# Running sums of squares of the norms: added by GpSimd instead of the vector engine, in a hybrid decoder layer on one core

## The chip, the core and the metric

The kernel runs on one core of a Trainium2 chip. The core has a matrix engine (TensorE, in the profile PE, its weight loads PEld), a vector engine (VectorE, DVE), an activation engine (ScalarE, ACT), a general engine (GpSimd, POOL) and a queue for transfers (SyncE, SP). Each engine works through its own list of instructions in order and waits only at semaphores. Operands lie in SBUF (128 partitions), products of TensorE in PSUM. The metric is the time of one execution on the device in microseconds; less is better.

## What is computed

One layer on 1056 tokens (1024 of a prompt, 8 x 4 new ones) with 1024 features: a feed-forward block, a mixer of two head groups (convolution and linear recurrence), a second feed-forward block, and a gated input embedding. Each block has an RMS norm before and after it.

```python
def rmsnorm(x, g):
    y = xf * lax.rsqrt(jnp.mean(xf * xf, axis=-1, keepdims=True) + EPS)
    return (y * g.astype(jnp.float32)).astype(x.dtype)

def decoder_layer(...):
    x = x + 0.5 * rmsnorm(swiglu_ffn(rmsnorm(x, ffn1_pre_g), ...), ffn1_post_g)
    x, ... = mixer_block(x, ...)      # pre2, conv norm, post2 inside: x + rmsnorm(out, post_g)
    x = x + 0.5 * rmsnorm(swiglu_ffn(rmsnorm(x, ffn2_pre_g), ...), ffn2_post_g)
    gate = jax.nn.sigmoid(rmsnorm(x, ple_norm_g) @ ple_w_gate)
    e = p @ ple_w_proj
    return x + rmsnorm(gate * e, ple_post_g)
```

## The kernel before

**Tiling.** Features lie on the partitions (8 tiles of 128), tokens along the free dimension in three chunks c = 0, 1, 2 of C = 352. Every tensor of x is 128 x 8 x 1056. All products are made in three passes (`passes`, L589 to L591) of a high and a low part, so each activation exists as `x_hi` (a rounded copy, ScalarE) and `x_lo` (the rest, VectorE), and each weight block as `w_hi` (ScalarE, L1022 or L1018) and `w_lo` (VectorE, L1503 or L1498).

**A norm.** A norm of one chunk needs the mean of squares over all features. ScalarE squares tile after tile (`square`, L1048): the first tile goes straight into the running sum `ssum[:, i % 2]`, the others into a ring `sq` of SQ = 3 buffers, so that square m waits for add m-3. `add_square` (L1526) adds each of them to the sum. TensorE adds over the partitions (`norm_sum`, L628), ScalarE takes the root (L1057), VectorE the reciprocal (`invert`, L1541), TensorE spreads it to all partitions (`norm_spread`, L640), and ScalarE copies it to `rstd_pre` or `rstd_post` (L1065). TensorE makes products between these steps. There are 27 norms, in the order of the table `NORMS`: pre1, then post1 and pre2, conv, post2 and pre3, post3 and pre4, post4, each for three chunks. They have 8 tiles (conv: 4), so 177 adds. Each add waits for its square and for the add before it; the counters `sq_done` and `add_done` run through all norms.

**Where VectorE makes the adds.** For pre1 it alternates `x_lo` (L1757) and an add. For a post-norm it makes the 7 adds in one row (`add_squares`), in the FFN's last step after the 8 sums of the chunk (`down`, L1650, acc = ps + acc). The pre-norm behind a post-norm is computed in `apply_pair`, four times per chunk, two tiles each: acc times rstd (L1554), times gain plus x_hi (L1559, twice), plus x_lo (L1563); then ScalarE makes the new x_hi (L1077) and squares the two tiles, and VectorE makes x_lo of the pair before (L1568) and the adds of that pair; in the last call it also serves its own pair. Where the next step of the program is a unit of the mixer, of w_out or of the gate, the calls stand between the units' instructions (gelu_in L2035, oc, L2154 and L2163). All these orders are written out by hand.

**GpSimd** makes three constants and the identity at the start (L565 to L569), then nothing.

**Waits on TensorE's side.** `norm_sum` waits for `add_done` to reach the last add of its norm, `norm_spread` for the reciprocal. Both stand in TensorE's list among the products, so a late add holds up all products behind it. `start_products` of chunk c waits tile by tile for x_lo.

Of the kernel before, what the change touches and what calls it, by code (L numbers as in the profile page):

```python
# [23 lines left out]
ALU = mybir.AluOpType  # L24
# [6 lines left out]
NJ = 4  # L31
# [16 lines left out]
SQ = 3  # L48
# [83 lines left out]
NORM = {(n, c): i for i, (n, c, _) in enumerate(NORMS)}  # L132
TILES = [t for _, _, t in NORMS]
BEHIND = [i for i, (n, _, _) in enumerate(NORMS) if not n.startswith("pre")]
SQ0 = [sum(TILES[:i]) for i in range(len(TILES) + 1)]
ADD0 = [sum(t - 1 for t in TILES[:i]) for i in range(len(TILES) + 1)]
# [55 lines left out]
def build(nc, a, out):  # L192
    ctx = ExitStack()
    with ctx:
# [24 lines left out]
        ssum = tile("ssum", [P, 2, C])  # L219
        std = tile("std", [P, 8])  # L220
        sq, sq_at, _ = place("sq", [P, SQ, C])
# [341 lines left out]
        @block.gpsimd  # L563
        def _(eng):
            eng.memset(ident[:, :], 0.0).then_inc(const_ready, 1)  # L565
            eng.memset(ones[:, :], 1.0).then_inc(const_ready, 1)
            eng.memset(eps_t[:, :], EPS).then_inc(const_ready, 1)
            eng.wait_ge(const_ready, 3)
            eng.affine_select(out=ident[:, :], in_=ident[:, :], compare_op=ALU.not_equal, fill=1.0,  # L569
                              base=0, pattern=[[-1, P]], channel_multiplier=1  # L570
                              ).then_inc(const_ready, 1)

# [891 lines left out]
        def _(eng):  # L1466
# [51 lines left out]
                eng.tensor_tensor(wd_lo[:, :], rawd[:, :], f32(wd_hi[:, :]), ALU.subtract  # L1518
                                  ).then_inc(down_lo, 1)

            def add_square(i, m):

                eng.wait_ge(sq_done, SQ0[i] + m + 1)
                if ADD0[i] + m - 1 > 0:
                    eng.wait_ge(add_done, ADD0[i] + m - 1)
                eng.tensor_tensor(ssum[:, i % 2, :], ssum[:, i % 2, :], sq[:, (ADD0[i] + m - 1) % SQ, :],  # L1526
                                  ALU.add
                                  ).then_inc(add_done, 1)

            def add_squares(name, c):  # L1530
                i = NORM[name, c]
                for m in range(1, TILES[i]):
                    add_square(i, m)

            def invert(name, c):

                i = NORM[name, c]
# [11 lines left out]
            def apply_pair(post, c, x0, src, gain, pre, q):  # L1549

                r, m, two = rstd(post, c), 2 * q, src(c, 2 * q, 2)
                n = mark(eng.tensor_tensor(two, two, r.unsqueeze(1).broadcast_to([P, 2, C]),  # L1554
                                           ALU.mult))
                eng.wait_ge(dve_own, n)
                for h in range(2):
                    t = src(c, m + h)[:, 0, :]
                    n = mark(eng.scalar_tensor_tensor(t, t, gain(m + h),  # L1559
                                                      f32(x_hi[:, m + h, cols(c)]),  # L1560
                                                      ALU.mult, ALU.add))
                eng.wait_ge(dve_own, n)
                eng.tensor_tensor(two, two, f32(x_lo[:, m:m + 2, cols(c)]), ALU.add  # L1563
                                  ).then_inc(x_new if pre else y_fin, 1)
                for p in ((q - 1, q) if q == 3 else (q - 1,)):
                    if pre and p >= 0:
                        eng.wait_ge(x_hi_done, x0 + PAIRS * c + p + 1)
                        eng.tensor_tensor(x_lo[:, 2 * p:2 * p + 2, cols(c)], src(c, 2 * p, 2),  # L1568
                                          f32(x_hi[:, 2 * p:2 * p + 2, cols(c)]), ALU.subtract
                                          ).then_inc(x_lo_done, 1)  # L1570
                        for k in (2 * p, 2 * p + 1):
                            if k:
                                add_square(NORM[pre, c], k)

            def scaled(f, i, c, h, up):

# [98 lines left out]
            def ffn_last(f, post, pre, x0):  # L1675


                i = NI - 1
                for c in range(NC):
                    def pair(q):  # L1680
                        if c:
                            apply_pair(post, c - 1, x0, acc_tile, half_gain(f), pre, q)

                    def hook(at):
                        if c == 0 and at == "g0":
                            split_down(i + NI * f)
                        if c and at == "g1":
                            invert(*((post, 0) if c == 1 else (pre, 0)))
                        if c == 2 and at == "u0":
                            invert(post, 1)  # L1690
                    hidden_chunk(f, i, c, tiles(f, i), hook)
                    pair(0)
                    for m in range(KT):
                        down(f, i, c, m)
                        if m in (2, 5, 7):
                            q = 1 + (2, 5, 7).index(m)
                            pair(q)
                            if c == 2 and q > 1:
                                for k in range(4):
                                    tiles(f, i)(1, 4 * (q - 2) + k)  # L1700
                    if (f, c) != (1, 2):
                        add_squares(post, c)

            def p_to_features():
                for c in range(NC):
# [46 lines left out]
            for c in range(NC):  # L1752
                i = NORM["pre1", c]
                for k in range(KT):
                    n = RING["xT", c, k]
                    eng.wait_ge(sq_done, SQ0[i] + k + 1)
                    eng.tensor_tensor(x_lo[:, k, cols(c)], ps[:, n % BANKS, 0:C],  # L1757
                                      f32(x_hi[:, k, cols(c)]), ALU.subtract
                                      ).then_inc(psum_free, 1)
                    eng.wait_ge(psum_free, n + 1)  # L1760
                    if k:
                        add_square(i, k)
                if c == 0:
                    vectors()
                    split_wide(0)
                    split_wide(1)
                invert("pre1", c)
                hidden_chunk(0, 0, c, tiles(0, 0),
                             lambda at: (c, at) == (2, "g0") and split_down(0))
# [300 lines left out]
            for n in range(12):  # L2070
# [10 lines left out]
                gelu_in(n)  # L2081
                if n:
                    yb(n - 1)
                if part == 1:
                    for j in range(1, NJ):
                        add_square(NORM["conv", c], j)
                if part == 3:
                    invert("conv", c)
                if part == 0 and c:
# [16 lines left out]
            for c in range(NC):  # L2106
                for q in range(4):
# [6 lines left out]
                        out_pair(c - 1, q - 1)  # L2114
                    if c and q == 3:
                        out_pair(c - 1, 3)
                add_squares("post2", c)


            def hook(c, at):  # L2120
# [49 lines left out]

            ple_unit(0, 0)
            invert("pre4", 1)
            add_squares("post3", 2)
            ple_unit(0, 1)
            invert("post3", 2)
            for q in range(4):
                apply_pair("post3", 2, 6 * PAIRS, acc_tile, half_gain(1), "pre4", q)
                ple_unit(*divmod(q + 2, 4))
            add_squares("post4", 0)
            ple_unit(1, 2)  # L2180
            invert("pre4", 2)
            ple_unit(1, 3)
# [1 line left out]
            ple_unit(2, 0)  # L2184
            finish(0, 0)
            finish(0, 1)
            add_squares("post4", 1)
            ple_unit(2, 1)
            invert("post4", 1)
            finish(0, 2)  # L2190
# [3 lines left out]
            finish(1, 0)  # L2194
            finish(1, 1)
            ple_unit(2, 3)
            add_squares("post4", 2)
            invert("post4", 2)
            finish(1, 2)
            finish(1, 3)  # L2200
# [41 lines left out]
```

## Time and profile before

| | |
|---|---|
| Time, median of 3 runs | 2345.52 us (2345.4 to 2349.55) |
| Profiled execution, span from the first to the last instruction | 2337.7 us |
| TensorE busy | 2158.0 us (92%), 13020 matmuls |
| VectorE busy | 1317.6 us (56%), 2620 instructions |
| ScalarE busy | 769.8 us (33%), 1500 instructions |
| GpSimd busy | 0.9 us, 8 instructions |
| Adds of the sums (L1526) | 92.6 us, 177 instructions |

The span is that of one profiled execution; the runs measure the whole execution on the device, so their median is 7.8 us above it. In the profile a row of instructions gives the start in us from the span's start, the time they took, engine, line, operation, output and inputs, shape and count; in brackets stands how long the engine had been idle before and what ended that. Equal instructions that follow each other are drawn together (x7), also where short gaps lie between them. "L1526" is a line of the kernel before; in the changed kernel the lines are other ones.

### The profile page before, as it was taken

The page shows a single profiled execution, that of the slowest core. Times are in us where ns is not written, and L with a number is a line of the kernel's source. Part 1 is how long each engine was busy: PE and PEld are TensorE (multiplying, and loading weights), DVE is VectorE, ACT ScalarE, POOL GpSimd, SP SyncE. Part 2 cuts the span into 40 slices and gives each one's busy share as a digit, 9 for nine tenths or more (in the row PEclk, how much of TensorE's full clock was granted, in tenths as well). Part 3 has the DMA queues.
Part 4 walks back from the last instruction along what each step waited for, and adds up shares of the span by engine and source line. Part 5 has one row for each costly group of instructions (what it writes and reads, how often), then busy time and mean ns, then how long its engine had stood idle before and what let it go on. Part 6 is the DMA issues. An engine that isn't in the chain of part 4 may idle for free. (4 is left out here: it accounts for less than half of the span.)

```text
span 2337.7 us, 34611 instructions
## 1 busy us (share of the span) xinstructions
PE 2158.0 (92%) x13020; PEld 2106.1 (90%) x13020; DVE 1317.6 (56%) x2620; ACT 769.8 (33%) x1500; POOL 0.9 (0%) x8
## 2 busy tenths in 40 slices
PE   5899999999999878999989689999999999995886
PEld 5899999999999878887789689999999999995886
DVE  4544444543445666988555764545434554557686
ACT  4311121221122333365575532212221121225563
POOL 0000000000000000000000000000000000000000
PEclk8999999999999889999999889999999999998897
DMA  4101111101111011100014201111101111102222
GB/s 149 37 28 45 54 54 54 54 27 35 45 54 54 1 45 41 46 1 19 19 38 144 91 1 55 55 54 54 45 18 45 54 54 54 54 1 73 72 91 75
DMA packets 92360, 116.15 MB, mean 50 GB/s; under 512 B 4596, under 2 KB 83704, under 8 KB 92282
## 3 DMA queue, kind: packets, MB, share of 16 engines
q1 hardware_dynamic: 91065, 110.79, 14.4%
q10 hardware_dynamic: 1216, 4.33, 0.6%
q8 instruction: 48, 0.79, 0.1%
q14 instruction: 31, 0.25, 0.0%
HBM read 110.15 MB, written 4.95 MB: 49 GB/s over the span
## 5 line engine op out<-in xcount | busy, mean ns | idle before, releaser
L589 PE MATMUL ps<-x_hi,w_lo 128*128 128x352 f32 x2688 | 883.2, 329 | 17.8 <-DVE w_lo L1503 8.8
L590 PE MATMUL ps<-x_lo,w_hi 128*128 128x352 f32 x2688 | 872.9, 325 | 0.0
L591 PE MATMUL ps<-x_hi,w_hi 128*128 128x352 f32 x2688 | 871.9, 324 | 0.0
L589 PEld LDWEIGHTS ps<-x_hi,w_lo 128*128 128x128 f32 x2688 | 514.6, 191 | 19.1 <-DVE w_lo L1503 9.5
L590 PEld LDWEIGHTS ps<-x_lo,w_hi 128*128 128x128 f32 x2688 | 515.3, 192 | 0.0
L591 PEld LDWEIGHTS ps<-x_hi,w_hi 128*128 128x128 f32 x2688 | 513.5, 191 | 0.0
L589 PE MATMUL ps<-a_hi,wd_lo 128*128 128x352 f32 x1104 | 361.6, 328 | 24.6 <-DVE a_lo L1600 11.6
L590 PE MATMUL ps<-a_lo,wd_hi 128*128 128x352 f32 x1104 | 357.7, 324 | 0.0
L591 PE MATMUL ps<-a_hi,wd_hi 128*128 128x352 f32 x1104 | 357.3, 324 | 0.0
L1650 DVE TENSOR_TENSOR acc<-ps,acc 128x352 f32<-128x352 f32 x480 | 249.3, 523 | 88.7 <-PE ps L591 82.8
L1583 DVE TENSOR_TENSOR tmp_u<-ps,rstd_pre 128x352 f32<-128x352 f32 x132 | 69.1, 524 | 370.7 <-PE ps L591 370.7
L1022 ACT ACTIVATE w_hi<-raw,params 128x256 fp32r<-128x256 f32 x512 | 213.6, 496 | 132.0 <-DMA raw<-in_ffn_w_gu_dram 109.1
L1503 DVE SCALAR_TENSOR_TENSOR w_lo<-raw,params,w_hi 128x256 fp32r<-128x256 f32 x512 | 225.8, 477 | 46.7 <-ACT w_hi L1022 46.7
L1089 ACT ACTIVATE tmp_s<-tmp_g 128x352 f32<-128x352 f32 x132 | 65.3, 498 | 552.1 <-DVE tmp_g L1583 552.1
L589 PEld LDWEIGHTS ps<-a_hi,wd_lo 128*128 128x128 f32 x1104 | 210.4, 191 | 27.6 <-DVE a_lo L1600 12.8
L590 PEld LDWEIGHTS ps<-a_lo,wd_hi 128*128 128x128 f32 x1104 | 210.9, 191 | 0.0
L591 PEld LDWEIGHTS ps<-a_hi,wd_hi 128*128 128x128 f32 x1104 | 210.1, 190 | 0.0
L1583 DVE TENSOR_TENSOR tmp_g<-ps,rstd_pre 128x352 f32<-128x352 f32 x132 | 68.5, 522 | 244.1 <-PE ps L591 230.0
L1098 ACT ACTIVATE a_hi<-tmp_a 128x352 fp32r<-128x352 f32 x132 | 59.9, 494 | 418.4 <-DVE tmp_a L1594 418.4
L829 PE MATMUL ps<-gp,diag 128*128 128x352 f32 (+1 forms) x360 | 108.8, 460 | 3.5 <-ACT diag L1284 3.5
L1526 DVE TENSOR_TENSOR ssum<-ssum,sq 128x352 f32<-128x352 f32 x177 | 92.6, 523 | 22.3 <-ACT sq L1048 9.5
L829 PEld LDWEIGHTS ps<-gp,diag 128*128 128x128 f32 x360 | 69.2, 194 | 38.1 <-issue 5.5
(172 smaller groups left out, 1678.2 us busy)
## 6 DMA issues: line engine op xcount, KB each, us to landing
raw<-in_ffn_w_gu_dram SPq DMA_DIRECT2D x88, 512.0 KB, 3.5
rawd<-in_ffn_w_down_dram SPq DMA_DIRECT2D x22, 1024.0 KB, 7.6
raw<-in_w_out_dram SPq DMA_DIRECT2D x24, 512.0 KB, 3.5
raw<-in_ple_w_gate_dram SPq DMA_DIRECT2D x24, 512.0 KB, 3.4
raw<-in_w_in_dram SPq DMA_DIRECT2D x16, 512.0 KB, 4.0
x_in<-in_x_prompt_dram ACTq DMA_DIRECT2D x6, 512.0 KB, 7.8
out_dram<-y_stage SPq DMA_DIRECT2D x6, 512.0 KB, 2.8
rawd<-in_ple_w_proj_dram SPq DMA_DIRECT2D x1, 1024.0 KB, 7.2
```

Source lines behind the costliest of these rows:

```text
L589: eng.matmul(dst, wl, xh, start=first, stop=False)
L590: eng.matmul(dst, wh, xl, start=False, stop=False)
L591: return eng.matmul(dst, wh, xh, start=False, stop=last)
L829: mm = eng.matmul(dst[:, 0:w], diag[:, tap, :], gp[:, j, at0:at0 + w], start=tap == 0, stop=tap == TP - 1)
L1022: ins = eng.activation(w_hi[s][:, sl], raw[:, sl], ACT.Copy, scale=vec(gain, k))
L1089: eng.activation(tmp_s[:, h, :], tmp_g[:, h, :], ACT.Silu).then_inc(silu_done, 1)
L1098: eng.activation(a_hi[:, h, cols(c)], tmp_a[:, h, :], ACT.Copy).then_inc(a_hi_done, 1)
L1503: ins = eng.scalar_tensor_tensor(w_lo[s][:, sl], raw[:, sl], vec(gain, k), f32(w_hi[s][:, sl]), ALU.mult, ALU.subtract)
L1526: eng.tensor_tensor(ssum[:, i % 2, :], ssum[:, i % 2, :], sq[:, (ADD0[i] + m - 1) % SQ, :], ALU.add).then_inc(add_done, 1)
L1583: eng.tensor_tensor((tmp_u if up else tmp_g)[:, h, :], src, rstd_pre[:, cols(c)], ALU.mult).then_inc(psum_free, 1)
L1650: eng.tensor_tensor(acc[:, m, cols(c)], src, acc[:, m, cols(c)], ALU.add).then_inc(psum_free, 1)
```

## The change

`add_square` moves to the GpSimd program, which gets one loop over all norms and tiles behind its constants. All calls of it on VectorE go, the function `add_squares` too, and with the calls in pre1 the wait of VectorE for its own x_lo. The semaphores and their counts are the same, so squares, sums and products wait for the same events.

```diff
 @block.gpsimd
+            def add_square(i, m):
+
+                eng.wait_ge(sq_done, SQ0[i] + m + 1)
+                if ADD0[i] + m - 1 > 0:
+                    eng.wait_ge(add_done, ADD0[i] + m - 1)
+                eng.tensor_tensor(ssum[:, i % 2, :], ssum[:, i % 2, :], sq[:, (ADD0[i] + m - 1) % SQ, :],
+                                  ALU.add
+                                  ).then_inc(add_done, 1)
+
+            for i in range(len(NORMS)):
+                for m in range(1, TILES[i]):
+                    add_square(i, m)
 @block.vector
-            def add_square(i, m):
-            def add_squares(name, c):
...
 def apply_pair
-                        for k in (2 * p, 2 * p + 1):
-                            if k:
-                                add_square(NORM[pre, c], k)
 def ffn_last
-                    if (f, c) != (1, 2):
-                        add_squares(post, c)
 pre1
-                    eng.wait_ge(psum_free, n + 1)
-                    if k:
-                        add_square(i, k)
 conv norm
-                if part == 1:
-                    for j in range(1, NJ):
-                        add_square(NORM["conv", c], j)
 mixer, gated embedding
-                add_squares("post2", c)
-            add_squares("post3", 2)
-            add_squares("post4", 0)
-            add_squares("post4", 1)
-            add_squares("post4", 2)
```

VectorE's list at the end of the first FFN, chunk 1, from the second `apply_pair` to the next products of the hidden layer, before:

```order
L1568 TENSOR_TENSOR x_lo<-acc,x_hi 128x2x352
L1526 TENSOR_TENSOR ssum<-ssum,sq 128x352 x2
L1650 TENSOR_TENSOR acc<-ps,acc 128x352 x2
L1554 TENSOR_TENSOR acc<-acc,rstd_post 128x2x352
L1559 SCALAR_TENSOR_TENSOR acc<-acc,half_g,x_hi 128x352 x2
L1563 TENSOR_TENSOR acc<-acc,x_lo 128x2x352
L1568 TENSOR_TENSOR x_lo<-acc,x_hi 128x2x352
L1526 TENSOR_TENSOR ssum<-ssum,sq 128x352 x2
L1568 TENSOR_TENSOR x_lo<-acc,x_hi 128x2x352
L1526 TENSOR_TENSOR ssum<-ssum,sq 128x352 x9
L1583 TENSOR_TENSOR tmp_g<-ps,rstd_pre 128x352 x2
```

and now:

```order
L1567 TENSOR_TENSOR x_lo<-acc,x_hi 128x2x352
L1646 TENSOR_TENSOR acc<-ps,acc 128x352 x2
L1553 TENSOR_TENSOR acc<-acc,rstd_post 128x2x352
L1558 SCALAR_TENSOR_TENSOR acc<-acc,half_g,x_hi 128x352 x2
L1562 TENSOR_TENSOR acc<-acc,x_lo 128x2x352
L1567 TENSOR_TENSOR x_lo<-acc,x_hi 128x2x352 x2
L1579 TENSOR_TENSOR tmp_g<-ps,rstd_pre 128x352 x2
```

The adds are gone from between the x_lo, and the nine at the end (two of pre2, seven of post1) no longer stand ahead of tmp_g. Near the end of the program, from the last unit of the gated embedding to the first pair behind the last norm, VectorE's list before:

```order
L2154 TENSOR_TENSOR acc<-ps,rstd_pre 128x352 x2
L2163 TENSOR_TENSOR acc<-ps,acc 128x352 x2
L1526 TENSOR_TENSOR ssum<-ssum,sq 128x352 x7
L1541 RECIPROCAL std<-std 128x3
L1554 TENSOR_TENSOR acc<-acc,rstd_post 128x2x352
```

and GpSimd's list now, from its last constant to its end:

```order
L567 MEMSET eps_t 128x1
L569 ISA
L569 AFFINE_SELECT ident<-ident 128x128
L578 TENSOR_TENSOR ssum<-ssum,sq 128x352 x177
L194 UNCONDITIONAL_BRANCH
```

VectorE's reciprocal now follows the unit directly and waits there for the sum, with the applies queued behind it as before; the adds stand in a list that holds nothing else.

## Rows read from the trace of the kernel before

**Rows 1.** The page: busy time of TensorE; its busy tenths and granted clock in 40 slices.
```profile
PE 2158.0 (92%) x13020; PEld 2106.1 (90%) x13020; DVE 1317.6 (56%) x2620; ACT 769.8 (33%) x1500; POOL 0.9 (0%) x8
...
PE   5899999999999878999989689999999999995886
...
PEclk8999999999999889999999889999999999998897
```

**Rows 2.** Adds (L1526) in five stretches: sum of the stretches, sum of busy time.
```profile
sum 785.00, DVE 92.62; mean DVE 18.52
```

**Rows 3.** Who waits for whom, TensorE: us in total, times, longest.
```profile
PE ps_aux L628 <- DVE ssum L1526: 71.9, 10, 11.8
```

**Rows 4.** Instructions of VectorE by form: busy us, mean ns, idle before.
```profile
L1650 DVE TENSOR_TENSOR acc<-ps,acc 128x352 f32<-128x352 f32 x480 | 249.3, 523 | 88.7 <-PE ps L591 82.8
...
L1526 DVE TENSOR_TENSOR ssum<-ssum,sq 128x352 f32<-128x352 f32 x177 | 92.6, 523 | 22.3 <-ACT sq L1048 9.5 <-DVE ssum L1526 0.9
...
L1554 DVE TENSOR_TENSOR acc<-acc,rstd_post 128x704 f32<-128x704 f32 x44 | 38.8, 882 | 7.9 <-ACT rstd_post L1065 7.9
```

**Rows 5.** GpSimd in order of time, two of its eight instructions.
```profile
0.74 0.20 POOL L565 MEMSET ident<- 128x128 f32 x1 [0.29 <-POOLq L2230]
...
1.35 0.29 POOL L569 TENSOR_SCALAR_AFFINE_SELECT ident<-ident 128x128 f32<-128x128 f32 x1 [0.23 <-POOL eps_t L567]
```

**Rows 6.** In order of time, pre1 chunk 1: ScalarE, VectorE, TensorE.
```profile
49.84 0.49 ACT L1190 ACTIVATE x_hi<-ps 128x352 fp32r<-128x352 f32 x1
50.52 0.51 ACT L1190 ACTIVATE x_hi<-ps 128x352 fp32r<-128x352 f32 x1
...
51.03 0.52 DVE L1526 TENSOR_TENSOR ssum<-ssum,sq 128x352 f32<-128x352 f32 x1
...
52.03 0.52 DVE L1526 TENSOR_TENSOR ssum<-ssum,sq 128x352 f32<-128x352 f32 x1
...
53.09 0.63 PE L589 MATMUL ps<-x_hi,w_lo 128*128 128x352 f32 x1 [1.18 <-DVE x_lo L1757]
```

**Rows 7.** In order of time, pre2 chunk 0: VectorE, ScalarE, TensorE.
```profile
797.33 0.52 DVE L1526 TENSOR_TENSOR ssum<-ssum,sq 128x352 f32<-128x352 f32 x1
797.76 1.38 DVE L1650 TENSOR_TENSOR acc<-ps,acc 128x352 f32<-128x352 f32 x3
...
802.70 1.15 DVE L1526 TENSOR_TENSOR ssum<-ssum,sq 128x352 f32<-128x352 f32 x2
803.76 0.95 DVE L1650 TENSOR_TENSOR acc<-ps,acc 128x352 f32<-128x352 f32 x2
...
810.14 5.55 DVE L1526 TENSOR_TENSOR ssum<-ssum,sq 128x352 f32<-128x352 f32 x9
...
808.28 1.04 ACT L1048 ACTIVATE sq<-acc 128x352 f32<-128x352 f32 x2
...
810.75 3.64 ACT L1048 ACTIVATE sq<-acc 128x352 f32<-128x352 f32 x6 [0.66 <-DVE ssum L1526]
...
818.40 0.26 ACT L1057 ACTIVATE std<-ps_aux,eps_t 128x3 f32<-128x3 f32 x1
...
811.34 1.44 PE L628 MATMUL ps_aux<-ones,ssum 128*128 128x1 f32 x6 [6.12 <-DVE ssum L1526]
...
819.37 0.81 PE L640 MATMUL ps_aux<-ident,std 128*128 128x128 f32 x6
```

**Rows 8.** In order of time, TensorE: behind pre2 chunk 2, behind conv chunk 1.
```profile
891.72 0.66 PE L589 MATMUL ps<-x_hi,w_lo 128*128 128x352 f32 x1 [6.16 <-DVE x_lo L1568]
...
1195.69 1.60 PE L640 MATMUL ps_aux<-ident,std 128*128 128x128 f32 x6 [5.77 <-DVE std L1541]
```

**Rows 9.** In order of time, TensorE: the sum of post3 chunk 2.
```profile
2178.25 1.44 PE L628 MATMUL ps_aux<-ones,ssum 128*128 128x1 f32 x6 [3.98 <-DVE ssum L1526]
```

**Rows 10.** In order of time, VectorE: the adds of post4 chunk 1.
```profile
2272.76 4.29 DVE L1526 TENSOR_TENSOR ssum<-ssum,sq 128x352 f32<-128x352 f32 x7
```

**Rows 11.** In order of time, VectorE: the adds of the last norm.
```profile
2305.49 4.30 DVE L1526 TENSOR_TENSOR ssum<-ssum,sq 128x352 f32<-128x352 f32 x7 [0.18 <-ACT sq L1048]
```

More of the change, by code:

```diff
@@ L1519, in split_down @@
                                   ).then_inc(down_lo, 1)
-            def add_square(i, m):
[L1523 to L1528, printed above, removed]
-            def add_squares(name, c):
-                i = NORM[name, c]
-                for m in range(1, TILES[i]):
-                    add_square(i, m)
             def invert(name, c):
```

## Prediction

> **What bounds the kernel now.** I read the page first, then who waits for whom on TensorE, then the instructions in order of time around those waits. TensorE is busy for 2158 of 2337.7 us, and its slices are at 9 or more except at the start, in slices 14 to 16, 21 to 24 and 37 to 40; the granted clock (PEclk) falls in most of the same slices [rows 1]. All adds lie in five stretches around these, together 785 us [rows 2]; the long loops of the two FFNs hold none. So the loops can't move, and the change is decided in the five stretches. There the largest single wait of TensorE is for the last add of a sum: 71.9 us in 10 waits [rows 3]. An add costs the vector engine 523 ns, 92.6 us for 177 of them [rows 4]. What matters is how much of these lies on a chain that TensorE waits for. All times below are walked from the trace of this one execution.
>
> **The price of an add on GpSimd.** No row shows it. GpSimd runs 8 instructions before, all at the start; the nearest are a memset of 128x128 in 0.20 us and a select over 128x128, which reads one operand, in 0.29 us [rows 5]. By length (352/128) they give 0.55 and 0.80 us. An add reads two operands; at worst the reads follow each other, 1.6 us. I take 0.9, nearest to the select, and a hand-off to the next add (each waits for the one before) of 0.1 as on the vector engine, where nine adds take 5.55 us, a pitch of 0.63 against 0.525 busy [rows 4, 7]. Pitch 1.0 us, ends 0.65 and 1.7.
>
> **Do the two engines hinder each other?** No row shows GpSimd beside the vector engine. The price is bounded below by nothing and above by one whole add for each add that meets a vector instruction with two SBUF operands. The vector engine takes 523 ns for an add of two SBUF tiles and 523 ns for one with a PSUM operand [rows 4], so it draws two SBUF streams at full rate; the question is whether GpSimd's two streams fit beside them. I take it that they don't and that the engines take turns, instruction by instruction: a third reader that needs two streams of its own is more likely to cost something than nothing, and the applies are made of just such instructions. Instructions with a PSUM operand run freely beside an add. The Trainium skill, "SBUF — State Buffer", section "Who interferes with whom", says the same in stronger words: a vector instruction with two SBUF inputs and a GpSimd instruction that reads SBUF exclude each other for the whole instruction. No run here shows it yet; if it is wrong, rival 1 is the sum.
>
> **Start: -1.7.** In chunks 1 and 2 of the first norm the vector engine alternates x_lo and add, 0.99 us per tile, while ScalarE makes a copy and a square in 0.69, and TensorE waits for x_lo before its products [rows 6]. These x_lo read PSUM and one SBUF tile, so there are no turns. Without the adds x_lo follows ScalarE. TensorE needs the first four x_lo; they come 1.0 us earlier in chunk 1 and 0.7 in chunk 2. The squares now wait for GpSimd (three buffers: square m waits for add m-3), at 1.0 per tile, no slower than 0.99 before. In chunk 0 the wait for parameters hides everything.
>
> **The nine pre-norm sums.** One walked, chunk 0 of pre2 [rows 7]. Removed from the vector engine ahead of the last pair's squares: one add and a pair, 0.43 and 1.06 of pitch = 1.49. Put in: adds 1 to 5 run on GpSimd as soon as their squares are there. Add 1 meets an apply, 0.9; of the pair 2, 3 and the pair 4, 5 one each hides under the L1650 instructions that read PSUM, and the others cost 0.75 and 0.6. Together 2.25 - 1.49 = +0.8. At the end: the two last squares finish at 809.3 + 0.8 = 810.1; GpSimd waits for the x_lo instruction that holds SBUF until 810.05 and adds twice, 812.1, against 811.3 before. TensorE's wait so ends 0.8 later. Then comes the post-norm behind it: its last square waits for its add 4, at 812.1 + 4.0, ends at 816.6 against 814.4, and ScalarE's silu and root stand behind it on its queue (a table load, silu and a second load; some 0.5 us of the delay is absorbed where silu waited for its input). The root comes at 820.1 instead of 818.4, the reciprocal at 820.6, and TensorE's spread at 820.8 instead of 819.4: **+1.4**. The same walk for the others with TensorE or its inputs waiting gives +1.5 and +1.2 in chunks 1 and 2 of pre2, +2.0, +2.1 and +0.9 for pre3, +2.0 and +1.7 for pre4 chunks 0 and 1; eight in all, +12.8. They differ by what covers the adds: a wait for w_hi covers some in chunk 1, nothing covers those of chunk 2, where TensorE waits for x_lo itself [rows 8]. The ninth, pre4 chunk 2, is made while the gate units run: its adds fall under sigmoids and PSUM readers, and the freed vector engine releases the next unit earlier, -2.6.
>
> **The conv norms: -1.3.** Three adds of 1.0 end 1.2 us later than three of 0.6, once on TensorE's path; but the y_lo and w_lo behind them on the vector engine start up to 1.7 us earlier, and TensorE waits for that chain 5.77 us before the next spread [rows 8]. In all -2.6 without turns; w_lo reads two SBUF tiles, which takes half of it back.
>
> **Post-norm sums of the last stage.** Where all squares are ready and nothing hides the adds, seven cost 7.0 instead of 4.3 us, +2.7. That is so for post3 chunk 2, where TensorE waits 3.98 us [rows 9], and for post4 chunk 2, the last norm of the kernel: add, sum, root, reciprocal, spread, applies and stores all stand in one chain behind it [rows 11]. In post4 chunk 0 the next unit is released 0.3 earlier. In post4 chunk 1 the seven adds stood behind two pairs of applies [rows 10]. They now start at 2266.6 instead of 2272.8, but run in turns with the applies, 5.7 us of two-operand instructions; six turns of 0.9 push the applies to 2278.2, and the unit behind them starts 1.2 later. Sum: 2.7 + 2.7 - 0.3 + 1.2 = +6.3. Queues: only GpSimd's gets work, nothing but adds, and in the order in which they ran before, so no norm is held up by a foreign one. The DMA queues of SP and ScalarE are not touched; ScalarE's squares wait for other times, which is counted above. Further shares of the 92.6 us lie in waits of the vector engine and bring nothing.
>
> **Sum:** -1.7 + 12.8 - 2.6 - 1.3 + 6.3 = +13.5 us. Span 2337.7 + 13.5 = 2351.2; the median of the runs is 7.8 above this span, so 2359. Per 0.1 us of pitch the sum moves by about 5 us (four post adds or two last adds in each of eight walks, and 2 x 7 at the end), since the last add is on the chain.
>
> **Rivals.** 1: *No hindrance.* The same walks with free adds: eight pre-norm sums -8.5, the ninth -2.8, conv -2.6, post3 +2.7, post4 -0.8, -4.0 and +2.7, start -1.7: -15, time 2330.5. Here the result is faster; it turns at a pitch of about 1.35 us. For it speaks that vector instructions keep 514 to 528 ns here while TensorE and ScalarE read SBUF beside them; against it, that neither of these reads as the vector engine does. 2: *Long adds.* A pitch of 1.6 or more (two reads one after the other, or a slow start of each instruction): the sum of the forecast + 6 x 5 = +43, time 2389. Against it speaks the select's 0.29. 3: *Nothing to measure.* Turns, but with a pitch near 0.8, or half as many collisions: the sum is 0 to +4, about 2347. The gains in the chunks where TensorE waits 6 to 12 us and the longer sums cancel. 4: *GpSimd starves.* If the vector engine's next instruction always goes first, the applies run as in rival 1, and the adds follow in one row at their end: three to four late adds in each of the eight walks, about +2.2 each, +18 in all with the end, 2364. It lies inside the forecast's band.
>
> **How the numbers follow.** Forecast with its neighbour 4: 0.58 (2352 to 2375). No hindrance: 0.22 (2324 to 2338). Nothing to measure: 0.13. Long adds: 0.07. About 0.2%, 4.7 us, is what a measurement of this kernel can tell from no change. Slower holds 0.56 of the first case, 0.07 of the long adds and 0.01 of the third; faster holds 0.21 of the second and 0.02 of the third; the rest is same. The whole range is 2327 to 2380: it reaches into both neighbours and leaves out the lower end of rival 1 and the long adds. The forecast's own range is 2350 to 2378.
>
> **What would show it.** Adds on GpSimd with a start-to-start spacing of 1.0 us, TensorE's waits for ssum near 85 us instead of 71.9. If the turns are real, the mean of L1554, L1563 and L1568 grows or gaps of up to 0.9 us open ahead of them, and L1650 keeps its 523 ns; if not, they stay at 0.88 us and the applies end 1.5 us earlier in each chunk. The last sum of the kernel must be 2.7 us longer in any case, and TensorE's products of chunks 1 and 2 must start about 1 us earlier. The forecast is wrong if the engines don't meet, or if the pitch is far from 1.0.

## The result, and the profile after

| | before | after |
|---|---|---|
| Time, median of 9 runs each | 2344.41 us (2335.91 to 2349.55) | 2355.28 us (2352.43 to 2363.84) |
| Span of the profiled execution | 2337.7 us | 2352.4 us |
| TensorE busy | 2158.0 us | 2162.9 us |
| VectorE busy | 1317.6 us | 1256.6 us |
| GpSimd busy | 0.9 us | 181.8 us |

The ratio of the times is 1.0054, 95% interval [1.0039, 1.0069]: about 12.7 us slower, between 9 and 16. Here and below, microseconds beside a ratio are the ratio times the median of the runs of before that it was measured against; the two medians of the table are 10.9 us apart. The two profiled executions are 14.7 us apart. The page of the changed kernel, busy time, then GpSimd's slices and the clock granted to TensorE:

```profile
PE 2162.9 (92%) x13020; PEld 2109.1 (90%) x13020; DVE 1256.6 (53%) x2443; ACT 766.8 (33%) x1500; POOL 181.8 (8%) x185
...
POOL 2100000000000230000012310000000000022131
PEclk8999999999999989999999799999999999997897
```

GpSimd works where the five stretches of [rows 2] lie, and nowhere else. VectorE lost 61 us of busy time, not the 92.6 us of its adds: 31.6 us are missing. Added up one by one, its 2443 other instructions take 26.6 us longer than before; the other 5 us are overlaps of neighbouring rows, which busy time counts once. 16.5 of the 26.6 us are to be seen in the instructions on `acc` (line, engine, form, count: min/median/max in ns, first and last start), which answer to [rows 4], with GpSimd's adds above them:

```profile
L578 POOL TENSOR_TENSOR ssum<-ssum,sq x177: 923/943/1987, 11.6 to 2323.5; 128x352 f32<-128x352 f32 x177
```
```profile
L1646 DVE TENSOR_TENSOR acc<-ps,acc x480: 510/524/526, 167.6 to 2159.3; 128x352 f32<-128x352 f32 x160
...
L1558 DVE SCALAR_TENSOR_TENSOR acc<-acc,half_g,x_hi x48: 571/584/1257, 784.2 to 2241.5; 128x352 f32<-128x352 f32 x48
L1553 DVE TENSOR_TENSOR acc<-acc,rstd_post x44: 858/884/1633, 783.3 to 2340.5; 128x704 f32<-128x704 f32 x44
L1562 DVE TENSOR_TENSOR acc<-acc,x_lo x44: 891/892/1524, 785.3 to 2342.6; 128x704 f32<-128x704 f32 x44
```

An add on GpSimd takes 0.93 us where it is alone. VectorE's instructions with two SBUF operands keep their medians, but their longest are 0.63 to 0.75 us above them (the longest L1554 before was 893 ns). The w_lo made of two SBUF tiles do the same (L1516: median 476 ns, longest 1199). L1646, which reads PSUM, has no long one among 480. So some instructions wait, each by up to most of one add.

TensorE's waits, the answer to [rows 3] (us in total, times, longest):

```profile
PE ps_aux L641 <- POOL ssum L578: 85.2, 13, 12.2
```

Chunk 0 of pre2, the answer to [rows 7], GpSimd first, then VectorE, ScalarE and TensorE:

```profile
797.80 2.48 POOL L578 TENSOR_TENSOR ssum<-ssum,sq 128x352 f32<-128x352 f32 x2 [3.09 <-ACT sq L1061]
803.38 6.63 POOL L578 TENSOR_TENSOR ssum<-ssum,sq 128x352 f32<-128x352 f32 x6 [3.09 <-ACT sq L1061]
```
```profile
798.10 1.40 DVE L1553 TENSOR_TENSOR acc<-acc,rstd_post 128x704 f32<-128x704 f32 x1
799.54 1.63 DVE L1558 SCALAR_TENSOR_TENSOR acc<-acc,half_g,x_hi 128x352 f32<-128x352 f32 x2
```
```profile
805.79 0.50 ACT L1061 ACTIVATE sq<-acc 128x352 f32<-128x352 f32 x1 [0.57 <-POOL ssum L578]
...
810.62 1.28 ACT L1102 ACT_TABLE_LOAD   x1
...
814.11 0.26 ACT L1070 ACTIVATE std<-ps_aux,eps_t 128x3 f32<-128x3 f32 x1
```
```profile
805.75 1.44 PE L641 MATMUL ps_aux<-ones,ssum 128*128 128x1 f32 x6 [6.70 <-POOL ssum L578]
814.63 0.91 PE L653 MATMUL ps_aux<-ident,std 128*128 128x128 f32 x6 [0.76 <-DVE std L1540]
```

Two adds that met applies took 2.48 us, the first six of a row of nine (two of pre2, seven of post1) 6.63. L1553 took 1.40 instead of 0.88. The sum waited 6.70 us instead of 6.12. Then ScalarE's squares of the post-norm behind (five of them alike) each wait 0.57 to 0.59 us for an add, since a square may only be written when the add three before it is done. Silu and root stand behind them on the same queue, and the spread comes when the root does.

The two ends that nothing covers, TensorE at post3 chunk 2 [rows 9] and GpSimd's adds of the last norm [rows 11]:

```profile
2191.56 1.44 PE L641 MATMUL ps_aux<-ones,ssum 128*128 128x1 f32 x6 [7.06 <-POOL ssum L578]
```
```profile
2317.09 7.34 POOL L578 TENSOR_TENSOR ssum<-ssum,sq 128x352 f32<-128x352 f32 x7 [30.53 <-ACT sq L1061]
```

7.06 us of waiting instead of 3.98, and seven adds in 7.34 us instead of 4.30.

**How the traces are compared below.** Each norm has a sum and a spread on TensorE (L628 and L640 before). The start of each, minus its start in the trace of before, is a shift; where the shift grows, time is lost between this step and the one before it. A shift belongs to two executions.

### The profile page after: what moved, and what is told of

The parts are those of the page before. It is cut to its first block and busy times, and to the rows that moved or that the text cites. A ratio compares the mean times of both kernels' runs of the same rounds, so it can differ in the third digit from the quotient of the medians.

```text
span 2352.4 us, 34607 instructions
## 1 busy us (share of the span) xinstructions
PE 2162.9 (92%) x13020; PEld 2109.1 (90%) x13020; DVE 1256.6 (53%) x2443; ACT 766.8 (33%) x1500; POOL 181.8 (8%) x185
## 5 line engine op out<-in xcount | busy, mean ns | idle before, releaser
L578 POOL TENSOR_TENSOR ssum<-ssum,sq 128x352 f32<-128x352 f32 x177 | 180.9, 1022 | 2141.9 <-ACT sq L1061 2123.7
L1646 DVE TENSOR_TENSOR acc<-ps,acc 128x352 f32<-128x352 f32 x480 | 249.3, 523 | 87.1 <-PE ps L604 81.2
L1516 DVE SCALAR_TENSOR_TENSOR w_lo<-raw,params,w_hi 128x256 fp32r<-128x256 f32 x512 | 229.1, 484 | 53.5 <-ACT w_hi L1035 53.5
L602 PEld LDWEIGHTS ps<-a_hi,wd_lo 128*128 128x128 f32 x1104 | 210.4, 191 | 24.8 <-DVE a_lo L1596 12.8
L641 PEld LDWEIGHTS ps_aux<-ones,ssum 128*128 128x128 f32 x162 | 27.3, 247 | 88.8 <-POOL ssum L578 88.8
```

Source lines behind the costliest of these rows:

```text
L602: eng.matmul(dst, wl, xh, start=first, stop=False)
L641: mm = eng.matmul(ps_aux[:, n % 2, q:q + 1], ssum[:, i % 2, t0:t0 + P], ones[:, 0:1], start=True, stop=True)
L1516: ins = eng.scalar_tensor_tensor(w_lo[s][:, sl], raw[:, sl], vec(gain, k), f32(w_hi[s][:, sl]), ALU.mult, ALU.subtract)
L1646: eng.tensor_tensor(acc[:, m, cols(c)], src, acc[:, m, cols(c)], ALU.add).then_inc(psum_free, 1)
```

## Experiments

The theory going in: what is lost is lost because each GpSimd add is longer, where it stands at the end of a chain, and because the two engines take turns when both read SBUF. Rivals: only the length matters; only the clock differs; nothing adds up because what one step gives another takes.

All mixes but the three with extra work use one rule, with VectorE's calls in their places as before and the same semaphore counts (where pre1 is on GpSimd, VectorE's wait for its own x_lo goes with its adds). Squares, sums and products are the same whoever adds:

```diff
+def on_gpsimd(i, m):
+    name, c, _ = NORMS[i]
+    return <the rule of the experiment>
 @block.gpsimd
+            for i in range(len(NORMS)):
+                for m in range(1, TILES[i]):
+                    if on_gpsimd(i, m):
+                        add_square(i, m)
 @block.vector
             def add_square(i, m):
+                if on_gpsimd(i, m):
+                    return
```

### One part at a time

**The sums of pre2, pre3 and pre4 alone.** Rule: `name in ("pre2", "pre3", "pre4")`.

> Only the sums of pre2, pre3 and pre4 (nine norms, 63 of the 177 adds) are added by GpSimd, all others by the vector engine as before. Theory (turns): the two last adds of eight of these sums end 0.8 us later as in the walk of pre2 chunk 0, but the post-norm sum behind each keeps its pitch of 0.63 us, so less than the +1.4 to +2.1 per norm is left: 8 x 0.6 - 2.6 for the ninth = about +2 us, and the vector engine's two-operand instructions show maxima of 1.3 us and more. Rival (no hindrance, length of the adds alone): 8 x -1.1 - 2.8 = about -11 us. Rival (collisions are the whole loss): as much slower as the changed kernel, +11 us.

Measured: ratio 0.9997 [0.9985, 1.0009], -0.7 us. Neither -11 nor +11: near the theory, at its favourable side. VectorE's other instructions together take 15.5 us longer than before, so the collisions are there, and still nearly nothing is lost. In this -0.7 us the ninth sum, pre4 chunk 2, is included, at which the shift falls by 3.0 us (below). So the other eight cost about 2 us, give or take as much, where the theory had 8 x 0.6 = 4.8.

**All post-norms and conv norms.** Rule: `name in ("post1", "post2", "post3", "post4", "conv")`.

> The complement of e1 and e4: GpSimd adds the sums of all post-norms and conv norms (93 adds), the vector engine those of pre1 to pre4. If the parts add up, it costs what is left of the changed kernel's 12.7 us: 12.7 + 5.2 + 0.7 = +18.6 us. Theory (the post-norm's root is late where its adds stand behind the pre-norm's on GpSimd, and the last sums are longer; with the pre-norm's adds back on the vector engine the post-norm's start no later than before): post3 chunk 2 +3.1, the last norm +3.0 to 4.5, eight post-norms behind a pre-norm up to 1.5 each, conv -0.6: +8 to +18, below the sum of the parts. Rival (post-norm sums are hidden but for the two at the end): +6.

Measured: 1.0067 [1.0050, 1.0085], +15.7 us, about 12 to 20. That excludes the rival of +6. With pre1 alone (-5.2, below) and the pre-norms alone (-0.7) the three parts add up to 9.8 us, the whole change to 12.7 with an interval of 9 to 16, so they add up within the noise. The two traces show how the loss divides. Chunk 0 of pre2, sum and spread on TensorE, first with the pre-norm's adds on GpSimd alone, then with the post-norms' alone:

```profile
811.09 1.44 PE L647 MATMUL ps_aux<-ones,ssum 128*128 128x1 f32 x6 [5.99 <-POOL ssum L583]
819.08 0.80 PE L659 MATMUL ps_aux<-ident,std 128*128 128x128 f32 x6
```
```profile
807.60 1.44 PE L647 MATMUL ps_aux<-ones,ssum 128*128 128x1 f32 x6 [6.12 <-DVE ssum L1547]
816.49 0.91 PE L659 MATMUL ps_aux<-ident,std 128*128 128x128 f32 x6 [0.72 <-DVE std L1562]
```

From sum to spread it is 8.03 us before [rows 7], 7.99 with the pre-norms on GpSimd, 8.89 with the post-norms, 8.88 in the changed kernel. The same subtraction at the five places where a post-norm's squares lie between the two steps, in us against before:

| sum to spread | changed kernel | pre-norms alone | post-norms, conv alone |
|---|---|---|---|
| pre2 chunk 0 | +0.85 | -0.04 | +0.86 |
| pre2 chunk 1 | +1.49 | -0.30 | +1.81 |
| pre3 chunk 0 | +1.93 | -0.61 | +1.90 |
| pre3 chunk 1 | +1.27 | -0.02 | +1.26 |
| pre4 chunk 0 | +1.28 | +0.17 | +1.29 |
| sum | +6.8 | -0.8 | +7.1 |

The growth of the shift up to the six sums of pre2 and pre3 is +1.3 us in the changed kernel, +1.6 with the pre-norms alone and +0.3 with the post-norms alone. So the longer pre-norm sums cost some 1.5 us in all six, and almost five times as much is lost behind them, where the post-norm's adds lie. The way there is ScalarE: its rows of waits name the squares (us in total, times, longest), pre-norms alone, then post-norms and conv alone:

```profile
ACT sq L1067 <- POOL ssum L583: 3.3, 8, 0.6
```
```profile
ACT sq L1067 <- POOL ssum L583: 22.1, 38, 1.1
```

In the changed kernel it is 25.4 us in 46 waits. The total alone says little, for the squares waited before too, for VectorE's adds:

```profile
ACT sq L1048 <- DVE ssum L1526: 19.6, 15, 6.0
```

Of these 19.6 us, 13.7 lie in three long waits (near 771, 2071 and 2273 us), where VectorE made its adds only after other work; the changed kernel has no such wait longer than 1.1 us, but 24 of its 46, 13.4 us, lie at the five places of the table. There the squares of a post-norm that follow each other are paced by the adds, 1.07 us instead of 0.6, and the root of the pre-norm's sum stands behind them. The direct test, a ring of six square buffers under the changed kernel, wasn't made: it needs three more buffers of 1408 bytes per partition each. So ScalarE's part rests on these rows and on the mixes.

**The first norm alone.** Rule: `name == "pre1"`.

> Only the sums of pre1, the first norm (three chunks, 21 adds), are added by GpSimd. By the walk TensorE's products of chunks 1 and 2 start about 2 us earlier and nothing else changes: -2 us. If the fall of the granted clock behind the wait for wd_lo near 100 us is missing here too, as in the trace of the changed kernel, -6 us. Rival (what comes earlier is waited for elsewhere): 0.

Measured: 0.9978 [0.9966, 0.9991], -5.2 us. In the trace chunk 2's sum comes 2.3 us earlier (about 2 were expected), and at the first post-norm the shift is -6.3. The other 4.1 us arise where the clock differs. TensorE's work from 90 to 110 us by stretches (start:end, length, busy us of PE, PEld, DVE, ACT, POOL, granted clock, DMA share, GB/s), before and then in the changed kernel, where the shift falls by the same 4.1 us:

```profile
90.00:100.00 10.00, 7.36 (x47) 7.07 (x46) 3.64 (x4) 4.40 (x5) 0.00 (x0) 0.93 0.00 0
100.00:110.00 10.00, 10.00 (x49) 10.00 (x49) 8.27 (x21) 5.99 (x15) 0.00 (x0) 0.73 0.17 52
```
```profile
90.00:100.00 10.00, 7.36 (x48) 7.07 (x47) 4.08 (x5) 6.15 (x9) 0.00 (x0) 1.00 0.00 0
100.00:110.00 10.00, 10.00 (x63) 9.73 (x62) 10.00 (x25) 4.24 (x10) 0.00 (x0) 1.00 0.28 80
```

In both, TensorE waits 2.6 us once for wd_lo in the first stretch. Behind it the clock granted is 0.73 before (part of the stretch at 1.2 instead of 2.4 GHz, 49 matmuls in 10 us) and 1.00 in the changed kernel (63 matmuls). How much of the 4.1 us the change gives is open: with the pre-norms alone on GpSimd, where all work up to 778 us is that of before, the clock is 0.92 in the second stretch and the shift falls by 1.2 us too, and in the last mix below, which has pre1 on GpSimd, it falls by 2.8. The two traces of before are the slowest of all in this piece.

**The first norm and the ninth pre-norm.** Rule: `name == "pre1" or (name, c) == ("pre4", 2)`, 28 adds.

> Only the sums of pre1 and of pre4 chunk 2 (28 adds) are on GpSimd. Theory (steps add up, each where its own vector instructions are freed): the 5.2 us that pre1 alone gave, and 2.6 to 3.0 for the ninth pre-norm, whose step was -2.9 in the changed kernel and -3.0 with the pre-norm sums alone: about -8 us against the kernel before. Rival (what one gives is taken back by a lower clock or a later wait): -5 us or less.

Measured: 0.9959 [0.9944, 0.9975], -9.6 us. The shift falls by 3.0 us at the spread of pre4 chunk 2 (-2.3 to -5.3), as it does in the changed kernel (14.1 to 11.1) and with the pre-norms alone (7.5 to 4.5). The steps add up.

### The ends

**The last norm back on VectorE.** Rule: `(name, c) != ("post4", 2)`.

> As the changed kernel, but the seven adds of the very last norm (post4 chunk 2) are back on the vector engine. Theory: nothing covers this sum, 7 x (1.05 - 0.615) = 3.0 us come back, so 0.13% less than the changed kernel, +8 us against the kernel before. Rival (something else in the tail grew, 4.5 us between the last units of the two traces): all of 4.5 us comes back. Rival (the loss is only the clock's): nothing comes back.

Measured: 1.0036 [1.0022, 1.0049] against 1.0054: 4.2 us come back by the two ratios, though their intervals overlap. The adds are again a row of VectorE's, of the old length:

```profile
2315.77 4.30 DVE L1547 TENSOR_TENSOR ssum<-ssum,sq 128x352 f32<-128x352 f32 x7 [0.18 <-ACT sq L1067]
```

From the spread of post4 chunk 1 to the last sum the shift grows by 1.2 us here and by 4.6 in the changed kernel: 3.4 us are this norm's. The other 1.0 to 1.2 appears in the kernels with pre1 alone and with pre1 and the ninth too, which change nothing there. It belongs to the trace of before, not to the change.

**The last two adds of every sum on VectorE.** Rule: `m < TILES[i] - 2`.

> In every sum the last two adds are made by the vector engine, all before them by GpSimd. Theory (the last adds of a sum stand on the chain and cost 1.05 instead of 0.6 us each): 0.9 us for the pre-norm sum in each of nine places, and as much for post3 chunk 2 and the last norm, come back: about 10 us less than the changed kernel, about 0 against the kernel before. Rival (collisions with the applies are the loss): they remain, at most 3 us come back, +8 us against the kernel before.

Measured: 1.0068 [1.0049, 1.0087]: no less than the changed kernel. My expectation fell, though the part it was about came true. The sum of pre2 chunk 0 waits 5.99 us instead of 6.70. What I hadn't walked is the queue behind the waiting add. GpSimd, VectorE, TensorE:

```profile
805.18 5.24 POOL L583 TENSOR_TENSOR ssum<-ssum,sq 128x352 f32<-128x352 f32 x5 [4.76 <-DVE ssum L1547]
```
```profile
810.53 1.16 DVE L1547 TENSOR_TENSOR ssum<-ssum,sq 128x352 f32<-128x352 f32 x2 [5.49 <-POOL ssum L583]
```
```profile
805.09 1.44 PE L647 MATMUL ps_aux<-ones,ssum 128*128 128x1 f32 x6 [5.99 <-DVE ssum L1547]
...
814.92 0.91 PE L659 MATMUL ps_aux<-ident,std 128*128 128x128 f32 x6 [2.89 <-DVE std L1562]
```

VectorE stands still for 5.49 us for the post-norm's fifth add, with tmp_g behind it in its queue. So silu and the root come late, and the spread waits 2.89 us instead of 0.76. A chain split between two engines makes the one that comes second wait with all that it has queued.

### Do the engines hinder each other?

Three kernels keep all adds on VectorE and give GpSimd extra work that no one waits for, released by the same squares. `op` is an add, a copy (each writes bf16, since no space for 352 fp32 elements is free), or four memsets:

```diff
+            idle = 0
+            for i in range(len(NORMS)):
+                for m in range(1, TILES[i]):
+                    eng.wait_ge(sq_done, SQ0[i] + m + 1)
+                    if idle:
+                        eng.wait_ge(idle_done, idle)
+                    op(...).then_inc(idle_done, 1)
+                    idle += 1
```

> The kernel before, with all 177 adds on the vector engine, and GpSimd beside them makes one add more for each, of 352 elements that belong to nobody (two reads of the constants ident, a write to a spare tile), released by the same squares. No work waits for them. Theory (turns between instructions that read two SBUF operands): the vector engine's adds and applies show maxima of 0.5 to 0.75 us above their medians, and since the adds themselves collide now too, the time rises by about 15 us (5 to 30). Rival (only the length of GpSimd's adds on the chain matters): 0, within 2 us.

> As with the extra adds, but each extra instruction is a copy of 352 elements: one SBUF read instead of two. Theory in its narrow form (only an instruction with two reads hinders): 0, within 2 us. In its wide form (any read of GpSimd hinders): in proportion to its busy time, half of the extra adds or more, +5 us and above, and maxima in the same rows.

> As with the extra adds, but four memsets of 176 elements in place of each add: GpSimd is busy for about as long and reads no SBUF. Theory: 0, within 2 us, and the vector engine's maxima stay within 20 ns of their medians. Rival (GpSimd's writes, or its semaphore traffic, are what hinders): as much as the extra adds.

| extra work on GpSimd | GpSimd busy | VectorE busy, against before | ratio | us |
|---|---|---|---|---|
| 177 adds (two SBUF reads) | 182.9 us | +82.9 us | 1.0348 [1.0326, 1.0370] | +81.6 |
| 177 copies (one SBUF read) | 103.1 us | +20.9 us | 1.0070 [1.0053, 1.0088] | +16.4 |
| 708 memsets (no read) | 174.8 us | -0.3 us | 1.0003 [0.9989, 1.0018] | +0.7 |

VectorE's own adds (min/median/max in ns) beside the extra adds, the copies and the memsets:

```profile
L1546 DVE TENSOR_TENSOR ssum<-ssum,sq x177: 509/1061/1291, 12.3 to 2394.5; 128x352 f32<-128x352 f32 x177
```
```profile
L1544 DVE TENSOR_TENSOR ssum<-ssum,sq x177: 511/609/798, 12.3 to 2326.8; 128x352 f32<-128x352 f32 x177
```
```profile
L1552 DVE TENSOR_TENSOR ssum<-ssum,sq x177: 515/525/528, 12.4 to 2316.1; 128x352 f32<-128x352 f32 x177
```

The work of all other engines is the same in all three, and so are its waits and counts. GpSimd busy without reads costs nothing that can be measured; a single read stream costs; two cost most. A copy is also shorter than an add (GpSimd is busy for 103.1 instead of 182.9 us), so the second read and the length aren't separated. The rows of the applies beside the extra adds:

```profile
L1574 DVE TENSOR_TENSOR acc<-acc,rstd_post x44: 859/884/1646, 789.8 to 2411.7; 128x704 f32<-128x704 f32 x44
```

So the hindrance is real, and it hangs on GpSimd reading SBUF. That it goes by whole instructions in turn fits these maxima (an add of 0.93 us lengthens no apply by more than 0.76) but isn't separated from a slowing of both. The narrow form of my theory (only two reads hinder) fell. The wide one holds in kind, but not in size: the copies cost a fifth of what the adds cost, not half, at 0.56 of their busy time. The cost of the extra adds I had wrong by a factor of five: I had counted the applies' collisions, but an extra add released by the same square meets VectorE's own add by construction, and that add's median doubles. The Trainium skill, "SBUF — State Buffer", section "Who interferes with whom", says that a VectorE instruction with two SBUF inputs contends with a GpSimd instruction that reads SBUF and not with one that only writes; these three kernels agree on each point. That the two exclude each other for the whole instruction, as the prediction has it from there, they leave open.

### How far two executions agree

> The kernel before once more, for a second trace. It tells how much of the shift between two traces is the execution's and how much the kernel's: if the granted clock between 906 and 1166 us follows from the work alone, TensorE reaches the first conv norm (1166.29 us) and the one before it (906.51 us) within 0.7 us of the same distance again, 259.8 us; in the traces with pre2's adds on GpSimd it was 263.4 to 265.2. Rival (the clock differs from execution to execution): the distance comes out anywhere between these.

> The changed kernel once more, for a second trace. If the granted clock follows from the work alone, every norm's step lies within 1 us of the first trace of it, the 5.4 us between 906 and 1166 us included (265.2 us from the spread of pre2 chunk 2 to the sum of conv chunk 0). Rival (the clock differs from execution to execution): between 259.8 and 265.2.

The second trace of before lies 0.3 to 0.6 us ahead of the first at every norm from 36 us to the end, the second of the changed kernel 0.6 to 1.8 us behind its first, 0.8 of it from the start. From the spread of pre2 chunk 2 to the sum of the first conv norm, in which no adds lie but the three of this sum, at its end: before,

```profile
905.91 0.81 PE L640 MATMUL ps_aux<-ident,std 128*128 128x128 f32 x6
1165.73 0.86 PE L628 MATMUL ps_aux<-ones,ssum 128*128 128x1 f32 x6 [4.12 <-DVE ssum L1526]
```

259.8 us as in the first trace; changed kernel, 265.05 us against 265.15:

```profile
905.32 0.81 PE L653 MATMUL ps_aux<-ident,std 128*128 128x128 f32 x6
1170.37 1.44 PE L641 MATMUL ps_aux<-ones,ssum 128*128 128x1 f32 x6 [5.64 <-POOL ssum L578]
```

Both values repeat. But the kernel with extra memsets, whose work on the path is that of before, needs 264.0 us for this piece, the one with pre1 alone 260.0, and the nine runs of before spread over 14 us. Of the 5.4 us of difference 1.5 are the longer sum (5.64 against 4.12 us of waiting); the other 3.9 lie where no add does, and I can't say by what rule they come. The long loop of the second FFN, from 1398 to 2078 us, moves too, though it holds no adds: by 0.1 and 1.2 us in the two traces of the changed kernel, by 3.4 with the pre-norms alone and 3.2 beside the memsets. So a shift of up to 4 us in such a piece doesn't by itself tell of the adds that were moved. What I can say is where the clock differs: between 960 and 980 us the clock granted is 0.91 before and 0.83 in the changed kernel, between 1120 and 1140 us 1.00 and 0.93.

### The version that follows from it

Give GpSimd the adds that free VectorE, and none that pace ScalarE or stand at an end:

```python
name == "pre1" or (name, c) == ("pre4", 2) or (name == "conv" and c > 0) \
    or (name in ("pre2", "pre3", "pre4") and m < TILES[i] - 2)
```

> GpSimd adds pre1, pre4 chunk 2, conv chunks 1 and 2, and of the other pre2, pre3 and pre4 sums all but the last two adds; the vector engine adds those two and all post-norm sums, so it never waits for a row of GpSimd's adds. Theory: pre1 -5.2, the pre-norm sums -0.7 as measured alone, the two last adds of eight of them 0.7 us each back, the conv norms -2.2: about -13 us, 0.9945. Rival (the collisions with the applies are what remains, and the clock takes the rest): as e9 or worse, -8 to 0.

Measured: 2329.75 us, ratio 0.9939 [0.9923, 0.9955], -14.3 us: faster than both kernels, by 0.6% than the kernel before and, by the two ratios, 1.1% than the changed one. The 28 adds of the mix before gave -9.6 us of it already, and the two intervals overlap, so that the other 46 adds gain anything isn't shown. Its steps in chunk 0 of pre2:

```profile
806.77 1.44 PE L648 MATMUL ps_aux<-ones,ssum 128*128 128x1 f32 x6 [5.91 <-DVE ssum L1548]
814.36 0.91 PE L660 MATMUL ps_aux<-ident,std 128*128 128x128 f32 x6 [0.80 <-DVE std L1563]
```

The shift up to the six sums of pre2 and pre3 now falls by 2.8 us in all, where it grew by 1.3 to 1.6, and from sum to spread at the five places it falls by 0.4 instead of growing by 6.8. The collisions remain (VectorE's other instructions take 16.0 us longer than before), so collisions of this size don't by themselves make a loss; in the changed kernel it is 26.6 us. ScalarE waits 0.8 us for GpSimd's adds instead of 25.4, and 15.4 for VectorE's, in six waits, most of it in the three long ones of before.

## Why the prediction came out right

I forecast 2359 us, 13.5 us more in the trace; it is 2355.28 us, and 14.7 more in the trace. The size is right partly by luck, as the terms show. All shifts are changed kernel against before, first trace of each.

**The price of an add**, 0.9 us and a pitch of 1.0: measured 0.93 and 1.07 (7.34 us for seven). By my slope of 5 us per 0.1 the sum would have been 3 to 4 us higher.

**Turns**: taken as likely; that the engines hinder each other is shown by the extra adds, copies and memsets. What I said of their form was too narrow: a GpSimd instruction with one read hinders too. The signs named ahead came: TensorE waits 85.2 us for the sums (near 85 forecast), the mean of L1554 rises from 882 to 950 ns (that of L1568 doesn't), and L1650 keeps its 523.

**Start, -1.7**: the products of chunks 1 and 2 came 1.5 and 2.2 us earlier. I had not foreseen the clock behind them, another -4.1 against this trace of before.

**Eight pre-norm places, +12.8.** Pre2: walked 4.1, measured 4.2. Pre3: walked 5.0, measured 3.5 and 2.9 more between the spread of chunk 0 and that of the post-norm behind it, where the clock granted is 0.67 from 1300 to 1310 us instead of 1.00. Those 2.9 us appear in the kernel with the post-norms alone too and not with the pre-norms alone. Where they appear with these, TensorE has just waited 1.8 to 1.9 us for the late spread of chunk 0, which it doesn't before; but with the last two adds of each sum on VectorE it waits 2.1 us there, and the clock doesn't fall. Pre4 chunks 0 and 1: walked 3.7, measured 2.4. The mechanism was the one walked, down to the squares that wait for the add three before. My heading for it was wrong: I called it the price of the pre-norm sums, but the experiments put most of it on the post-norm's adds, whose pace holds ScalarE. All pre-norm adds alone on GpSimd cost nothing that can be measured, the gain of the ninth included; without it, about 2 us. The prediction also said that the loops of the FFNs can't move; they moved by up to 3.4 us in single traces.

**The ninth, -2.6**: measured -3.0 in each kernel that has it.

**Conv, -1.3**: the first sum waits 1.5 us longer, and from there to the sum of post2 behind them the shift falls by 2.1: -0.6. The 5.4 us of shift that arise ahead of it (906 to 1166 us) were in no term; 1.5 of them are the longer sum, the rest lies in a stretch without adds.

**Ends, +6.3**: post3 chunk 2 walked +2.7, measured +3.1. Post4 chunk 1 walked +1.2, measured -0.8 (the sum waits 3.36 us instead of the 4.80 of before): the adds started as early as walked. The answer to [rows 10], five of GpSimd's seven adds (all seven take 9.02 us) and the first and last apply beside them:

```profile
2279.71 6.84 POOL L578 TENSOR_TENSOR ssum<-ssum,sq 128x352 f32<-128x352 f32 x5
```
```profile
2278.68 1.63 DVE L1553 TENSOR_TENSOR acc<-acc,rstd_post 128x704 f32<-128x704 f32 x1
...
2287.46 0.89 DVE L1562 TENSOR_TENSOR acc<-acc,x_lo 128x704 f32<-128x704 f32 x1
```

The two pairs of applies take 9.7 us instead of 5.8. I had priced six turns at 5.4; they cost 3.9.

The last norm: walked +2.7, measured +3.4.

**What offset what.** Unforeseen: -4.1 near 100 us, +3.9 in 906 to 1166 us, +2.9 near 1306, +1.1 ahead of the last norm. Their sum is +3.8. The terms that I priced came out at +9.9 instead of +13.5, and 1 us lies in small steps between the norms. The total agrees better than the terms do.

**The rivals.** No hindrance (-15) fell by the extra adds. Long adds fell by the 0.93 us. Nothing to measure fell by the interval, 9 to 16 us against its 0 to 4. GpSimd starving: the long L1553 and the 2.48 us for a pair show that both sides wait, so neither always goes first.

## What to carry to other kernels

An instruction that leaves a busy engine brings only what its place frees, and costs its longer duration only where someone is paced by it. So don't move a kind of instruction, move places: here 28 of the 177 adds on GpSimd make the kernel 0.4% faster, 74 of them 0.6%, and all 177 make it 0.5% slower. Look for the ring of buffers that ties the producer to the slower consumer, and for what else stands in the producer's queue behind it. And before giving GpSimd work beside VectorE, ask whether both read SBUF at the same moment; here, where the same event released both, they did so nearly each time.

## What the runs showed of the hardware

- A GpSimd add over 128x352 fp32 in SBUF takes 0.93 us, with 1.07 us from one to the next that waits for it; on VectorE it is 0.525 and 0.63.
- While it runs, a VectorE instruction with two SBUF operands is up to 0.75 us longer, and an add on VectorE released with it takes 1.06 us in the median instead of 0.525. Beside GpSimd copies such an add on VectorE takes 0.61 us in the median, beside memsets 0.525 as alone. VectorE instructions with one operand in PSUM and one in SBUF keep their 523 ns.
- GpSimd waits too: its longest add took 1.99 us.
- TensorE waits 2.6 us near 100 us in every kernel and is busy for 7.4 us of the ten before 100 in all but one. Behind that the clock granted from 100 to 110 us is 0.73 and 0.76 in the two traces of before, 0.92 in the trace with the pre-norms alone, whose work up to there is that of before, 0.83 beside the memsets, and 1.00 in both traces of the changed kernel. What decides it stays open.
